# Expert weights fetched as four runs of 4 KB per partition in place of one run of 16 KB

## The reference

```
xr = x_pad[row_tok].reshape(n_blocks, 128, d)      # tokens gathered by expert
def expert_block(args):
    xb, e = args
    h = silu(xb @ w_gate[e]) * (xb @ w_up[e])      # (128, 1024) @ (1024, 512)
    return h @ w_down[e]                           # (128, 512) @ (512, 1024)
y = segment_sum(out * row_w[:, None], row_tok)     # rows weighted and added up by token
```

## Time and profile before

| | us |
|---|---|
| median of 3 runs | 2915.01 |
| lowest and highest | 2914.62, 2915.88 |
| span of the profiled execution | 2913.0 |
| PE busy | 2454.0 (84%) |
| DVE busy | 1855.0 (64%) |
| ACT busy | 1480.3 (51%) |
| POOL busy | 650.8 (22%) |
| share of the 16 DMA engines' time, SP's queue q1 | 48.1% |
| the same, POOL's queue q0 | 3.1% |

### The profile page before, as it was taken

The page is one execution under the profiler, slowest core; times in us unless marked ns, Lnnn a source line. Parts: engine busy times, 40 slices in busy tenths (PEclk is TensorE's granted clock), DMA queues, the critical chain, the costliest instruction groups (busy, mean ns, idle before and its releaser), DMA issues. The chain is left out here.

```text
span 2913.0 us, 38772 instructions
## 1 busy us (share of the span) xinstructions
PE 2454.0 (84%) x12692; PEld 2074.2 (71%) x12692; DVE 1855.0 (64%) x2702; ACT 1480.3 (51%) x1774; POOL 650.8 (22%) x524
## 2 busy tenths in 40 slices
PE   5788998897499999998189999999955999999960
PEld 4667787786388888886178888888854888888850
DVE  2444455544688888886834444444456888888857
ACT  2333334422277777774334444444213777777742
POOL 0002344412123333221410000000121332223315
PEclk8899999998699999999589999999977999999985
DMA  7510000033399999996511111101243999999953
GB/s 140 71 36 22 22 22 22 28 91 141 114 367 369 365 370 368 372 375 257 202 46 31 36 34 38 45 31 53 71 160 139 370 378 378 380 368 362 360 229 163
DMA packets 128068, 540.57 MB, mean 186 GB/s; under 512 B 35840, under 2 KB 76816, under 8 KB 101392
## 3 DMA queue, kind: packets, MB, share of 16 engines
q1 hardware_dynamic: 108256, 504.73, 48.1%
q0 software_dynamic: 18432, 33.60, 3.1%
q10 hardware_dynamic: 1328, 1.59, 0.5%
HBM read 515.21 MB, written 58.20 MB: 197 GB/s over the span
## 5 line engine op out<-in xcount | busy, mean ns | idle before, releaser
L265 DVE TENSOR_TENSOR arena<-arena,arena 128x2048 fp32r<-128x2048 f32 (+1 forms) x438 | 923.7, 2145 | 134.5 <-ACT arena L1519 82.9
L1519 ACT CAST arena<-arena 128x2048 fp32r<-128x2048 f32 x380 | 704.9, 1917 | 189.1 <-PE psum L1313 97.4
L1313 PE MATMUL psum<-arena,arena 128*128 128x512 f32 x3072 | 737.0, 395 | 8.1 <-DVE arena L265 8.1
L1313 PEld LDWEIGHTS psum<-arena,arena 128*128 128x128 f32 x3072 | 571.2, 189 | 124.4 <-issue 5.6
L481 PE MATMUL psum<-arena,arena 128*128 128x512 f32 x2016 | 471.0, 395 | 45.5 <-ACT arena L581 43.7
L481 PEld LDWEIGHTS psum<-arena,arena 128*128 128x128 f32 x2016 | 383.2, 191 | 129.2 <-ACT arena L581 46.7
L1324 PE MATMUL psum<-arena,arena 128*128 128x512 f32 x1536 | 368.0, 395 | 9.2 <-DVE arena L265 9.2
L265 DVE TENSOR_TENSOR arena<-psum,arena 128x512 fp32r<-128x512 f32 (+2 forms) x244 | 200.8, 828 | 241.9 <-ACT arena L604 93.3
L1324 PEld LDWEIGHTS psum<-arena,arena 128*128 128x128 f32 x1536 | 288.1, 189 | 84.2 <-DVE arena L265 24.2
L256 PE MATMUL psum<-ident,arena 128*128 128x128 f32 x1152 | 179.7, 298 | 151.9 <-POOL arena L833 69.6
L256 PEld LDWEIGHTS psum<-ident,arena 128*128 128x128 f32 x1152 | 164.7, 198 | 180.9 <-POOL arena L833 78.4
(11 more groups left out here) (147 smaller groups left out, 2132.3 us busy)
## 6 DMA issues: line engine op xcount, KB each, us to landing
arena<-in_moe_w_gate SPq DMA_DIRECT2D x64, 2048.0 KB, 10.7
arena<-in_moe_w_up SPq DMA_DIRECT2D x64, 2048.0 KB
arena<-in_moe_w_down SPq DMA_DIRECT2D x64, 2048.0 KB, 9.1
arena<-expert_rows SPq DMA_DIRECT2D x16, 1024.0 KB, 14.5
x_rows<-arena SPq DMA_DIRECT2D x24, 512.0 KB, 4.9
arena<-x_rows SPq DMA_DIRECT2D x24, 512.0 KB, 5.8
arena<-in_c_w_in SPq DMA_DIRECT2D x24, 512.0 KB, 5.5
arena<-in_x SPq DMA_DIRECT2D x16, 512.0 KB, 4.2
```

What stands on the lines that cost most here:

```text
L265: return eng.tensor_tensor(tile, src, high.bitcast(F32), ALU.subtract)
L1313: mm = pe.matmul(bank(o), cs[:, c * P:(c + 1) * P], ws[:, c * FF:(c + 1) * FF], start=(k == 0 and c == 0), stop=(k == 2 and c == CH - 1))
L1519: act.copy(w_hi[w][:, cols], self.raw[w][:, cols]).then_inc(hi_ready[w], 1)
```

## The change

Every fetch of an expert matrix still moves the same 2 MB into the same slot with one DMA, but as four runs of 4 KB per partition. For gate and up, chunk c = 2a + j is the rows 256a + 2p + j; for down, chunk a is the rows 128a + p. The matmuls are the same in number, shape and SBUF addresses. The transposes follow the new order: the token rows are turned with a stride of 2 elements in place of 8, the hidden values without a stride in place of 4. The other phases keep their layout and their transposes.

```diff
         def transpose_group(pe, dst_bank, rows, c0, n, stride):
             for j in range(n):
-                m = pe.transpose(dst_bank[:, j * P:(j + 1) * P], rows[:, c0 + j:rows.shape[1]:stride], ident[:])
+                cols = slice(j * P, (j + 1) * P) if stride == 1 else slice(c0 + j, rows.shape[1], stride)
+                m = pe.transpose(dst_bank[:, j * P:(j + 1) * P], rows[:, cols], ident[:])
             return m
...
-                self.src = [moe_w_gate[layer].rearrange("e (p c) f -> e p (c f)", c=CH),
-                            moe_w_up[layer].rearrange("e (p c) f -> e p (c f)", c=CH),
-                            moe_w_down[layer].rearrange("e (p c) n -> e p (c n)", c=FCH)]
+                self.src = [moe_w_gate[layer].rearrange("e (a p j) f -> e p a (j f)", a=4, j=2),
+                            moe_w_up[layer].rearrange("e (a p j) f -> e p a (j f)", a=4, j=2),
+                            moe_w_down[layer].rearrange("e (a p) n -> e p a n", a=4)]
...
-                sp.dma_start(self.raw[w], self.src[w][bass.ds(e, 1)].rearrange("o p n -> (o p) n")
+                sp.dma_start(self.raw[w].rearrange("p (a n) -> p a n", a=4),
+                             self.src[w][bass.ds(e, 1)].rearrange("o p a n -> (o p) a n")
                              ).then_inc(sem if sem is not None else self.raw_in[w], 16)
...
                 def turn_rows(pe, b):
-                    for g in range(2):
-                        mm = transpose_group(pe, bank(B_XT + g), rows[b], 4 * g, 4, CH)
+                    for c in range(CH):
+                        first = 2 * P * (c // 2) + c % 2
+                        mm = pe.transpose(bank(B_XT + c // 4)[:, (c % 4) * P:(c % 4 + 1) * P],
+                                          rows[b][:, first:first + 2 * P - 1:2], ident[:])
                     return mm
...
-                            transpose_group(pe, bank(B_HT), hid, 0, FCH, FCH).then_inc(ht_ready, 1)
+                            transpose_group(pe, bank(B_HT), hid, 0, FCH, 1).then_inc(ht_ready, 1)
```

More of the change, by code:

```diff
@@ L1500, in more @@
                         pe.wait_ge(x_h, 1 + j + 1)
-                        transpose_group(pe, bank(B_HT), hid, 0, FCH, FCH).then_inc(x_ht, 1)
+                        transpose_group(pe, bank(B_HT), hid, 0, FCH, 1).then_inc(x_ht, 1)
                         pe.wait_ge(x_htl, 1 + j + 1)
```

## The result

The changed kernel takes 2935.93 us (median of 4 runs, 2933.22 to 2937.19), the kernel before in the same comparison 2915.45: a ratio of 1.0065, interval 1.0051 to 1.0079, or +19 us (15 to 23). It is slower, the side on which I had put 0.23, and lies outside my range of 2902 to 2932. The spans of the profiled executions are 2935.4 and 2913.0 us. From the first gather of a layer to the next phase's first transfer there are 637.6 us in place of 624.1 in layer 0 and 634.5 in place of 625.0 in layer 1; before, between and behind them nothing moved by over 0.4 us. So all of it is in the two expert phases.

The account below looks back on a forecast made before the run. The prediction took PE to bound the kernel, with transfers just ahead. Its sum was span 2913.0 + 1 - 6.0 - 0.5 = 2907.5, plus 2.0 from span to timed median: 2909.5 us, range 2902 to 2932.

Parts of the forecast that it names:

- the side on which I had put 0.23: Whole kernel: the chance given to the change making it slower, against 0.37 faster and 0.40 same.
- What bounds the kernel: Expert phases: PE, 98% busy, sets the pace, and the transfers arrive just ahead of their use.
- Step 1: Expert matrix fetches: service rises from 4.90 to 5.12 us, +0.22 us a matrix, +0.67 us a step.
- Step 2: Steady expert steps: gate lands up to 0.67 us later, within 1.0 us of room; +1 us for both layers.
- the term of +1 us: Steady expert steps: cost of a few more late landings, both layers together.
- The upper bound of +42 us: Steady expert steps: the whole 0.67 us paid in each of 62 refilled steps.
- a queue that falls behind wins back what the smaller packets cost: Fetch queue: a second queued fetch shows no start cost; a lone one lands after 7.6 us with 4.9 of service.
- Step 3: Start of each expert phase: first gather lands earlier behind smaller refill packets, gaining 3.0 us a layer, 6.0 in all.
- The second estimate there: First gather: if queues take turns by groups of 9 to 17 descriptors, a layer gains 2.8 us at most.
- The step's upper bound of 9.4 us: First gathers: 4.7 us lost to the up refill regained in each layer.
- Step 4: Transposes in 64 expert steps: smaller strides make weight loads faster, mostly hidden; -0.5 us in all.
- The slower rival: Gate refill in the steady part: late transfers take over, lateness adds up, about 2933 us; chance 0.23.

Follow-up runs that it names:

- e6: Kernel before, each refill of down fetching 12 KB of the 16 KB of a partition: 2917.42 us, ratio 1.0009.
- e1: Kernel before with only the fetches changed (four runs of 4 KB, 512 KB apart), transposes as before: 2937.37 us, ratio 1.0073.
- e7: Kernel before with one wait more on SP: first refill of up issued when the first gather has landed: 2906.50 us, ratio 0.9972.
- e2: Kernel before with only the transposes changed (stride 2 for token rows, none for hidden values), fetches as before: 2918.86 us, ratio 1.0009.
- e5: Changed kernel, each refill of down leaving out the fourth of its four runs: 2924.74 us, ratio 1.0038.
- e4: Kernel before with only the fetches changed, to one DMA of two 8 KB runs 1 MB apart: 2929.08 us, ratio 1.0047.
- e10: As e4, but the two runs fetched by two DMAs of one run each: 2916.95 us, ratio 0.9999.
- e3: Kernel before, its 16 KB cut into four neighbouring 4 KB runs by a reversed destination, transposes taking matching columns: 2932.65 us, ratio 1.0062.
- e9: Changed kernel, each matrix fetched by four DMAs of one 4 KB run a partition, same packets and addresses: 2911.35 us, ratio 0.9985.
- e11: Changed kernel, gathers and scatters moving no rows but index 0, expert_rows filled in the load phase: 2928.72 us, ratio 1.0049.
- e12: Kernel before with the same edit as e11: 2934.20 us, ratio 1.0065.
- e14: Changed kernel with two DMAs a matrix, each two runs of 4 KB a partition: 2924.96 us, ratio 1.0026.

## Why the prediction was wrong

- **What bounds the kernel** was right: PE, with the transfers just ahead. e6 shows it.
- **Step 1** was right in size: +0.22 us of service a matrix predicted, +0.17 measured in the steady part.
- **Step 2 failed**, in the sentence "It will land up to 0.67 us later". That took the landing as the mean engine's service. The landing belongs to the last of 16 engines, and with several runs in a DMA the engines lie 2.4 to 3.5 us apart in place of 1.8 to 2.7. Gate landed 1.2 us later by the median, past its 1.0 us of room, and up 1.6 us later in the mean. So the term of +1 us was really some 20 (e1: +21). The room was also read at a single step: the earlier trace rows had gate late already in 7 of some 29 steps, which had no room at all. I also looked at the room of gate alone; up, which I had not checked, was the other one that became late (22.9 us of waits, 5.3 before). The upper bound of +42 us would have held it, but I drew the range by the likely cases.
- That **"a queue that falls behind wins back what the smaller packets cost"** was no help: a matrix takes 0.5 to 0.6 us beyond the pure rate in both layouts (5.47 less 4.90, 5.64 less 5.12).
- **Step 3** had the right place and the wrong size: -0.8 us a layer in place of -3.0. The gather is really held by the refill (e7 wins 4.3 us at PE's start), but the two queues do not take turns by packet from the start: the first row of the gather came 3.7 us after POOL's issue behind four runs in one DMA, and 3.9 behind one. Four DMAs let it start after 1.8 to 1.9 us, and PE's waits for first rows fell by 6.7 us in both layers (37.9 to 31.2), about what this step had hoped for. The second estimate there, "2.8 us at most", took 9 packets a turn before and 17 after; with one number for both it is 4.1 to 7.7 us, so it was no bound. The step's upper bound of 9.4 us for both layers is nearly what e7 reached by taking the refill away (-8).
- **Step 4** missed by sign and is small: -0.5 us predicted, +3 measured in e2. I had taken the pace of a stride of 8 for that of a stride of 2.
- **The slower rival** named the place (gate, in the steady part), the point (1.0 us of room) and 2933 us, 3 us from the result. Its cause, that lateness adds up by service time, is not what e5 and e4 showed, and its price took half of the 0.67 us by choice, so that the number came so near is luck. The rule on row pitch of the Trainium skill (DMA: Bandwidth & Descriptors, Latency and other measured facts) played no part. It is about the pitch from partition to partition, and no run here has such a pitch: e10, whose runs within a partition are 1 MB apart, is at 0.9999, and neighbouring runs in one DMA (e3) lose 18 us.

**What is shown, and what stays open.** Shown: the loss needs several runs a partition in one DMA (e9, e10 against after, e4) and the rows of gathers and scatters beside it (e11 against e12, with e5 as the control for capacity). The late completion of some of the 16 engines goes with the loss in each kernel of the table under e14. Not shown: why an engine with a DMA of several runs falls back further when it also serves POOL's queue. The trace names no engine for a packet. An expert has 64 of 128 slots filled on average, so perhaps only half of the engines carry rows. The gap between the eighth and the ninth completion of gate, which is there before and after the change and gone without rows (e11), fits that; but with four DMAs (e9) it is gone too, with the rows moving, and no run spread the rows otherwise. Nor was the number of DMAs separated from the order of packets: one DMA of four runs may serve the pieces of its partitions in another order than four DMAs do.

## What to carry to other kernels

A fetch is late when its slowest engine is late, so next to its mean service look at the time from its first completion to its last, above all where a second queue (gathers, scatters) shares the engines. Where runs in HBM must be split and such a queue runs beside them, try one DMA a run and count the semaphore, rather than one DMA with several runs: here that was worth 23 us (1.0065 against 0.9985) for one loop in the code, 5 of them at the first gathers. Without rows in the second queue there was nothing to win (e11). And a transfer that nobody needs soon should not be issued in front of the one that starts the phase (-8 us for one wait).

## What was not expected of the hardware

- The same packets at the same addresses: one DMA of four runs +19 us, four DMAs -4 us (e9); two runs +14 and 0 us (e4, e10).
- Four times the DMAs did not slow PE, although SP issued four in 1.9 us in place of one in 0.33. PE's idle time ahead of down is 3.8 us in 440 in e9, and 3.8 in e2, which has the same transposes and one DMA a matrix.
- A gather that stands behind a fetch starts by the size of that DMA, not of its packets: 3.9, 3.2 and 1.8 us behind one, two and four DMAs for the same 2 MB, 0.7 us alone (layer 0).
- PE's pace over transposes of float32 depends on the stride unevenly. From the start of one transpose to the next in a group it is 109 ns by the median with a stride of 8 and without a stride, and 120 ns with strides of 2 and 4 (before and after, 800 to 1300 us). Eight take 1.04 us with a stride of 8 and 1.11 with a stride of 2. The weight loads of eight turns with a stride of 8 are 188 ns by the median (at 915.5 us before; the 192 of the earlier trace rows is over several strides). With a stride of 2 they are:

```profile
L1336 PEld LDWEIGHTS psum<-ident,arena x512: 194/209/231, 770.5 to 2807.7; 128*128 128x128 f32 x171
```
